# RWKV and gated delta cores: the inverse of the triangular blocks mirrored, with Y and X^T products on all four quarters of the array

## What is computed

```python
def step(state, inp):
    r_t, w_t, k_t, v_t, kk_t, b_t = inp
    sk = jnp.einsum('bhvk,bhk->bhv', state, kk_t)
    state = (state * w_t[:, :, None, :] - sk[..., None] * b_t[:, :, None, :]
             + v_t[..., None] * k_t[:, :, None, :])
    return state, jnp.einsum('bhvk,bhk->bhv', state, r_t)
```

```python
lower = jnp.where(strict, jnp.einsum('bhnid,bhnjd->bhnij', kb, k) * decay, 0.0)
tinv = lax.linalg.triangular_solve(eye + lower, eye, left_side=True, lower=True, unit_diagonal=True)
u = tinv @ (v * beta[..., None])
w = tinv @ (kb * jnp.exp(gcum)[..., None])
def step(S, inp):
    qd, kd, ui, wi, ai, gl = inp
    v_new = ui - wi @ S
    o = qd @ S + ai @ v_new
    S = S * gl[..., None, None] + jnp.einsum('bhcd,bhce->bhde', kd, v_new)
    return S, o
```

## Time and profile before

| | |
|---|---|
| median of 3 runs | 3152.23 us (3150.76 to 3156.98) |
| span of the profiled execution | 3153.8 us |
| PE busy / PEld busy | 2975.0 us (94%) / 2086.0 us (66%) |
| DVE / ACT / POOL busy | 1542.3 / 588.5 / 865.3 us |
| RWKV core | about 1036 to 1310 us of the span |
| gated delta core | about 2308 to 2515 us of the span |
| L2154, inverse products of RWKV | 3072 records, 115.4 us busy, 227 ns each |
| L3243, those of gated delta | 2688 records, 92.7 us busy, 222 ns each |

### The profile page before, as it was taken

How to read it: one execution, slowest core, us unless ns; L and a number is a source line. 1 busy time by engine, 2 the same in 40 slices (tenths; PEclk the granted TensorE clock), 3 DMA queues, 4 the chain that set the end, 5 groups by cost and what they waited for, 6 DMA issues and landing times. The chain is left out here.

```text
span 3153.8 us, 52317 instructions
## 1 busy us (share of the span) xinstructions
PE 2975.0 (94%) x22150; PEld 2086.0 (66%) x22150; DVE 1542.3 (49%) x2520; ACT 588.5 (19%) x1102; POOL 865.3 (27%) x591
## 2 busy tenths in 40 slices
PE   9999999999999899999999998999879998999998
PEld 6845857986887688658566685677768844443433
DVE  5764756336555467534777664764644332111112
ACT  2142040012001333210100002221443211110101
POOL 1111222111121545211899790011245310000000
PEclk9999999999999899999999999999999998999999
DMA  4342223220321000042334452132200017999996
GB/s 165 94 165 77 80 82 113 81 80 28 127 87 47 3 3 4 36 135 74 126 127 148 155 164 80 56 102 68 74 9 3 22 60 271 381 409 409 409 409 272
DMA packets 122230, 412.64 MB, mean 131 GB/s; under 512 B 13568, under 2 KB 21376, under 8 KB 121744
## 3 DMA queue, kind: packets, MB, share of 16 engines
q1 hardware_dynamic: 112784, 373.64, 33.3%
q0 software_dynamic: 9216, 35.66, 3.4%
HBM read 404.97 MB, written 4.28 MB: 130 GB/s over the span
## 5 line engine op out<-in xcount | busy, mean ns | idle before, releaser
L947 PE MATMUL ps<-arena 128*128 128x256 f32 x4760 | 1044.3, 381 | 18.0 <-PEq L905 6.8
L947 PEld LDWEIGHTS ps<-arena 128*128 128x128 f32 x4760 | 898.8, 191 | 173.9 <-issue 43.9
L1003 PE MATMUL ps<-arena 128*128 128x512 f32 (+1 forms) x752 | 291.5, 546 | 10.4 <-DVE arena L1342 7.3
L885 POOL TENSOR_TENSOR arena<-arena 128x512 f32<-128x512 f32 x68 | 94.1, 1384 | 555.9 <-DVE arena L903 190.5
L1003 PEld LDWEIGHTS ps<-arena 128*128 128x128 f32 x752 | 144.3, 193 | 149.6 <-issue 138.7
L3895 PE MATMUL ps<-arena 128*64 128x512 f32 x1024 | 224.8, 594 | 9.7 <-DMA arena<-in_w_up 7.2
L891 POOL TENSOR_TENSOR arena<-arena 128x512 f32<-128x512 f32 x68 | 86.5, 1271 | 484.7 <-PE ps L947 484.7
L1247 DVE TENSOR_TENSOR arena<-ps,arena 128x256 f32<-128x256 f32 x85 | 36.1, 425 | 331.1 <-PE ps L947 330.1
L1178 DVE SCALAR_TENSOR_TENSOR arena<-ps,params,arena 128x511 f32<-128x511 f32 (+4 forms) x266 | 190.7, 717 | 13.5 <-ACT arena L1079 4.4
L4039 POOL TENSOR_SCALAR arena<-arena,small 128x1024 f32<-128x1024 f32 x64 | 191.5, 2992 | 10.1 <-DMA arena<-in_w_mod 6.4
L3895 PEld LDWEIGHTS ps<-arena 128*64 128x64 f32 x1024 | 83.7, 137 | 149.2 <-issue 148.8
(11 more groups left out here) (453 smaller groups left out, 4047.6 us busy)
## 6 DMA issues: line engine op xcount, KB each, us to landing
arena<-in_w_in SPq DMA_DIRECT2D x166, 512.0 KB, 3.7
arena<-in_w_gate SPq DMA_DIRECT2D x128, 512.0 KB, 15.5
arena<-in_w_up SPq DMA_DIRECT2D x128, 512.0 KB, 15.3
arena<-in_w_down SPq DMA_DIRECT2D x128, 512.0 KB, 15.4
arena<-in_w_mod POOLq DMA_DIRECT2D x48, 512.0 KB, 4.2
arena<-in_ffn_up SPq DMA_DIRECT2D x44, 512.0 KB, 4.0
arena<-in_w_branch SPq DMA_DIRECT2D x32, 512.0 KB, 3.6
arena<-spill POOLq DMA_DIRECT2D x16, 640.0 KB, 5.3
```

The lines of the kernel that those rows point to most:

```text
L885: vec.tensor_tensor(plane(u, n), part(u, 1, 0), part(u, 1, 1), ALU.add).then_inc(sem, 1)
L947: last = nc.tensor.matmul(k.bank(b)[:, 0:HT], lhs[:, q * P:(q + 1) * P], rhs[:, q, :], start=(first and q == 0), stop=(q == 3), skip_group ...
L1003: last = nc.tensor.matmul(out[0:j["m"], 0:j["n"]], w[:, q * m:(q + 1) * m], j["rhs"](q), start=(n == 0), stop=(n == kn - 1))
```

## The change

In both cores the product is mirrored: a level now makes Y from XT, not from X, and XT from X and Y; X from Y and X. The order in a level is Y, XT, X. Y and XT (with X0, Y5 and XT5) are written so that the eight cells of one half of the partitions go to both halves and to two banks (`to_heads`, `to_chunks`; `to_tiles` in the gated delta core), round all four quarters. X (`in_heads`, `in_tiles`) stays on two, and takes a bank of its own: bank 6 in RWKV, which the norms, the turn of O and the bonus product use, with new waits between them and X; bank 7 in gated delta, where `chunk_u` moves too, with waits for X before each `chunk_u` and for its reader before X. The other steps there have banks 2, 3 and 4, and Y5, XT5 and X0 take two of them. RWKV's LT product is made twice, once each way round (banks 2 and 3, columns 0 to 255 and 256 to 511), since both orientations are wanted; in gated delta the LT step goes and an XT0 step comes. Readers of two banks read them in one instruction (`pair`, `both`). RWKV's turn of O moves from beat 10 to 9, the weighing from 12 to 10, the bonus from 14 to 13, its reader from 15 to 14; Y5 comes ahead of trv, which moves to beat 1, trkap from 2 to 4, trkt from 4 to 5.

The diff, cut to its core:

```diff
--- before.py
+++ after.py
@@ rwkv_core_phase
-    A = ["X0"] + [f"{s}{n}" for n in (1, 2, 3, 4) for s in ("Y", "X", "XT")]
-    B = ["trv", "Y5", "trkap", "XT5", "Lk", "trkt", "LkV", "trbt", "NU0", "WT", "Ak", "Ab"]
-    B_BEAT = [0, 0, 2, 2, 3, 4, 5, 6, 6, 7, 9, 11]
-    B_BANKS = [(3,), (2,), (3,), (2,), (2, 3), (3,), (2,), (3,), (2,), (2, 3), (2, 3), (2, 3)]
+    A = ["X0"] + [f"{s}{n}" for n in (1, 2, 3, 4) for s in ("Y", "XT", "X")]
+    B = ["Y5", "trv", "XT5", "Lk", "trkap", "trkt", "LkV", "trbt", "NU0", "WT", "Ak", "Ab"]
+    B_BEAT = [0, 1, 2, 3, 4, 5, 5, 6, 6, 7, 9, 11]
+    B_BANKS = [(2, 3), (2,), (2, 3), (2, 3), (2,), (3,), (2,), (3,), (2,), (2, 3), (2, 3), (2, 3)]
+    X_BANK = 6
     LT_BEAT = 13
+    TURN_BEAT, WEIGHED_BEAT, BONUS_BEAT, ADDED_BEAT = (9, 7), (10, 12), (13, 11), (14, 15)
@@
-            def blocks64(l, r, b):
-                for h in range(2):
+            def to_heads(l, r, b):
+                for i in range(TT):
+                    for q, h in ((0, 0), (1, 1), (0, 1), (1, 0)):
+                        other = k.const("ident")[half(q), half(q)] if r is None else r[half(q), cell(h, i)]
+                        ins = nc.tensor.matmul(k.bank(b + q)[half(h), 64 * i:64 * i + 64], l[half(q), cell(h, i)], other, start=True, stop=True)
+                return ins
+
+            def to_chunks(l, r, b):
+                for i in range(TT):
+                    for h, q in ((0, 0), (1, 1), (0, 1), (1, 0)):
+                        t = turned_cell(q, i)
+                        ins = nc.tensor.matmul(k.bank(b + h)[half(q), 64 * i:64 * i + 64], l[half(h), t], r[half(h), t], start=True, stop=True)
+                return ins
+
+            def in_heads(l, r, b):
+                for q in range(2):
                     for i in range(TT):
-                        for q in range(2):
-                            other = k.const("ident")[half(q), half(q)] if r is None else r[half(q), cell(h, i)]
-                            ins = nc.tensor.matmul(k.bank(b)[half(q), cell(h, i)], l[half(q), cell(h, i)], other, start=True, stop=True)
+                        for h in range(2):
+                            t = turned_cell(q, i)
+                            ins = nc.tensor.matmul(k.bank(b)[half(h), t], l[half(h), t], r[half(h), t], start=True, stop=True)
                 return ins
@@ step_a
-                    pe.wait_ge(*a_out(p, f"X{n - 1}"))
-                    ins = blocks64(LM(p), X(p), b)
+                    pe.wait_ge(*a_out(p, f"XT{n - 1}" if n > 1 else "X0"))
+                    ins = to_heads(LM(p), XT(p), 0)
...
-                    ins = blocks64(Y(p), XT(p), b)
+                    ins = to_chunks(X(p), Y(p), 0)
...
-                    ins = blocks64(XT(p), Y(p), b)
+                    if n == 1:
+                        pe.wait_ge(kap_ok, min(p + 2, PAIRS))
+                        if p >= 1:
+                            pe.wait_ge(*a_out(p - 1, "X4"))
+                    else:
+                        pe.wait_ge(*a_out(p, f"X{n - 1}"))
+                    if p >= 3 and n == 3:
+                        pe.wait_ge(weighed, p - 2)
+                    if p >= 3 and n == 4:
+                        pe.wait_ge(bonus_ok, p - 2)
+                    ins = in_heads(Y(p), X(p), X_BANK)
@@ step_lt
-                products(pl(a + p), pl(sg + p), 2).then_inc(lt_made, 1)
+                products(pl(a + p), pl(sg + p), 2)
+                products(pl(sg + p), pl(a + p), 2, 256).then_inc(lt_made, 1)
@@ the loop of PE
-                    if b >= 4 and beat == (10 if b < BLOCKS - 1 else 7):
+                    if b >= 4 and beat == TURN_BEAT[b == BLOCKS - 1]:
                         pe.wait_ge(norm_ok, b - 3)
                         pe.wait_ge(kap_ok, min(b + 1, PAIRS))
+                        pe.wait_ge(*a_out(min(b - 1, PAIRS - 1), "X2" if b < PAIRS + 1 else "X4"))
...
                         turn(O(b - 4), 6, k.const("swap")).then_inc(turned, 1)
-                    if b >= 4 and beat == (14 if b < BLOCKS - 1 else 11):
+                    if b >= 4 and beat == BONUS_BEAT[b == BLOCKS - 1]:
                         pe.wait_ge(weighed, b - 3)
                         pe.wait_ge(rk_ok, 2 * (b - 3))
+                        if b < PAIRS + 1:
+                            pe.wait_ge(*a_out(b - 1, "X3"))
                         nc.tensor.matmul(k.bank(6), HS, SQ(b - 4), start=True, stop=True).then_inc(bonus_in, 1)
@@ DVE, step_a and step_lt
+                if s[1] == "T":
+                    nc.vector.tensor_tensor(pair(x), pair(x), both(0), ALU.subtract).then_inc(a_dve, 1)
+                else:
+                    nc.vector.tensor_tensor(x, x, k.bank(X_BANK), ALU.subtract).then_inc(a_dve, 1)
...
-                nc.vector.tensor_tensor(quad(LT(p)), two_banks(2), mask(strict), ALU.mult).then_inc(lt_read, 1)
+                nc.vector.tensor_tensor(quad(XT(p)), two_banks(2), mask(first_level), ALU.mult)
+                nc.vector.tensor_tensor(quad(LS(p)), two_banks(2, 256), mask(after), ALU.mult).then_inc(lt_read, 1)
                 dve.wait_ge(lt_read, p + 1)
-                link(nc.vector.scalar_tensor_tensor(out=eight(XT(p)), in0=eight(LT(p)), scalar=-1.0, in1=mask8(level(0)), op0=ALU.mult, op1=ALU.mult))
-                nc.vector.tensor_tensor(eight(XT(p)), eight(XT(p)), mask8(ident), ALU.add).then_inc(lt_out, 1)
+                nc.vector.tensor_tensor(eight(XT(p)), mask8(ident), eight(XT(p)), ALU.subtract).then_inc(lt_out, 1)
@@ gdn_phase
+    X_BANK = 7
-    A = [f"{s}{n}" for n in (1, 2, 3, 4) for s in ("Y", "X", "XT")]
+    A = [f"{s}{n}" for n in (1, 2, 3, 4) for s in ("Y", "XT", "X")]
-    PREPARE = {0: ["R"], 4: ["KK"], 7: ["LT"], 9: ["QK"], 12: ["X0"]}
+    PREPARE = {0: ["R"], 4: ["KK"], 9: ["QK"], 10: ["XT0"], 12: ["X0"]}
+    TWO_BANKS = ("W", "Y5", "XT5", "X0")
-    BANKS = (2, 3, 7)
+    BANKS = (2, 3, 4)
-        n = 2 if step[0] == "W" else 1
-        banks_of[step] = [BANKS[(turn + i) % 3] for i in range(n)]
+        choices = ((2, 3), (3, 4)) if step[0] in TWO_BANKS else ((2,), (3,), (4,))
+        idle_since = lambda banks: max(ORDER.index(last_user[b]) if b in last_user else -1 for b in banks)
+        banks_of[step] = min(choices, key=idle_since)
@@ SP
+            sp.wait_ge(m_made, made_at("XT5", 4))
@@ step_a, X
+                    if n > 1:
+                        pe.wait_ge(*a_out(f"X{n - 1}", g))
+                    elif g >= 1:
+                        pe.wait_ge(*a_out("X4", g - 1))
+                    if g >= 3 and g % 2 == 1:
+                        pe.wait_ge(vn_ok, 4 * ((g - 3) // 2) + n)
+                    ins = in_tiles(X_BANK, Y(g), X(g))
@@ chunk_u
+                g = 2 * u + 3
+                if g < GROUPS:
+                    pe.wait_ge(*(a_out(f"X{n}", g) if n else a_out("X4", g - 1)))
+                elif n == 0:
+                    pe.wait_ge(*a_out("X4", GROUPS - 1))
-                        ins = nc.tensor.matmul(k.bank(4)[rows(z), wide(h)], ...
+                        ins = nc.tensor.matmul(k.bank(X_BANK)[rows(z), wide(h)], ...
```

More of the change, by code:

```diff
@@ L2027, in rwkv_core_phase @@
     own = lambda n: pl(at_plane[n])
-    LT, LM, X, XT, Y = (lambda p, n=n: own(5 * (p % 2) + n) for n in range(5))
+    LS, LM, X, XT, Y = (lambda p, n=n: own(5 * (p % 2) + n) for n in range(5))
     KT_, BT_, VT, NU, AK, AB = (lambda p, n=n: own(10 + 6 * (p % 2) + n) for n in range(6))
@@ L2138, in products @@
                         t = chunk(i, q)
-                        ins = nc.tensor.matmul(k.bank(b + h)[half(q), 64 * i:64 * i + 64], l[half(h), t], r[half(h), t], start=True, stop=True)
+                        ins = nc.tensor.matmul(k.bank(b + h)[half(q), at + 64 * i:at + 64 * i + 64], l[half(h), t], r[half(h), t], start=True, stop=True)
                 return ins
@@ L2386, in step_a @@
                 act.wait_ge(a_made, a_made_at(p, s))
-                nc.scalar.activation(Y(p) if s[0] == "Y" else X(p), k.bank(A.index(s) % 2), ACT.Copy).then_inc(a_act, 1)
+                nc.scalar.activation(pair(Y(p) if s[0] == "Y" else X(p)), both(0), ACT.Copy).then_inc(a_act, 1)
             def step_b(p, s):
@@ L3643, in _ @@
                         scaled(b - 2)
-                    if b < GROUPS and beat == 10:
+                    if b < GROUPS and beat == 8:
                         start(b)
```

163 lines of the change are left out of this document (96 added, 67 removed).

## The result

| | before | after |
|---|---|---|
| median, same chip and hour | 3156.61 us (3150.76 to 3161.19, 18 runs) | 3160.51 us (3153.80 to 3167.67, 18 runs) |
| ratio | | 1.0016, 95% interval 1.0008 to 1.0023 |
| span of the profiled execution | 3153.8 us | 3160.8 us |
| RWKV core, first scan to last gate product | 350.4 us | 366.3 us |
| gated delta core, first to last product that its function issues (its fills for the next phase among them) | 336.8 us | 322.9 us |

The change costs 5 us (2.5 to 7.3), which is inside the 0.2% that I had called "same", but on the other side of my forecast (2 us faster). Behind it stand two larger numbers of opposite sign. The windows of the profile after, answering, show them; columns as there. Blocks run from scan to scan of DVE in the RWKV core and from R product to R product in the other.

The account below looks back on a forecast made before the run. PE looked like the bound of both cores, though RWKV blocks change hands between ACT, DVE and PE. RWKV +8.1 and gated delta -11.0 gave -2.9, so 3152.2 became 3149.3; 0.7 for the clock made 3150 us, range 3133 to 3165.

Parts of the forecast that it names:

- same: Rival (a), whole kernel: the two cores' effects cancel, 3150 us, own range 3144 to 3157; chance 0.35.
- the last term of the sum: Whole kernel: more pauses of PE lower the clock, 0.7 us added to 3149.3.
- Rival (d): Full blocks and blocks 1 to 4: each loses one more half-clock stretch, 8 x 1.75 = 14 us, 3164; chance 0.19.
- six products x 0.38 less LT 0.62 and less a turn: RWKV block 2, behind the Lk mask: PE-bound saving of 1.1 us, the turn taken as 0.5.
- Beats 8 to 12: RWKV full block: turn of O, now in beat 9, waits for X2's subtraction, +1.15 us.
- Beat 12 to the results: RWKV full block: bonus product, now in beat 13, waits for X3's subtraction and delays LT, +2.3 us.
- The start of the block: RWKV blocks 5, 6, 7: later Y1 start (+0.4), product savings and a moved turn (+0.55) together give 0.0.
- rival (b): RWKV beats 8 to 15: earlier DVE subtraction hides the X2 and X3 waits, 14.5 us less, 3135; chance 0.32.
- my bounds of 1.8 to 3.3 for the second: Gated delta block 4: chunk_u's second wait for X's subtraction, behind DVE's XV and XK products, put at 2.5 us.
- (c): Rival, PE products: independent tiles bring a product to 0.50 us, another 8 us saved, 3142; chance 0.03.
- (e): Rival, gated delta: copies out of PSUM become the bound and its 11 us stay away, 3161; chance 0.06.
- (f): Rival, new products: they miss 0.63 us because operands lie differently; no saving, all waits stay, 3180; chance 0.05.

Follow-up runs that it names:

- gated delta alone: The kernel before with only the gated delta core of the changed kernel: 3147.42 us against 3154.95, ratio 0.9977.
- RWKV alone: The kernel before with only the RWKV core of the changed kernel: 3169.78 us, ratio 1.0047.
- output work moved only: The kernel before with only the turn of O, weighing, bonus product and its use moved to the changed kernel's beats, old products kept: 3165.61 us, ratio 1.0032.
- both back: The changed kernel with turn of O back in beat 10 (weighed in 11) and bonus product in 14 (used in 15): 3148.15 us, ratio 0.9973 to before.
- products in pairs: The changed kernel with matmuls of Y, XT and X0 going over two quarters at a time instead of four, both cores: 3185.21 us, ratio 1.0098 to before.
- second profile: The changed kernel run once more, unaltered, for its profile: 3151.38 us in this single run.
- the turn back: The changed kernel with only the turn of O back in beat 10 (weighed in 11), bonus product left in 13: 3155.75 us, ratio 1.0006 to before.

## Why the prediction was right or wrong

**The cause of the sign.** My sum was -2.9, +8.1 for RWKV and -11.0 for gated delta. In the profiles they are +15.9 and -13.9, in the timed runs of one core at a time +14.8 and -7.3. The mechanisms were those I named. What turned the sign is the clock, for which the sum had 0.7 us: the changed kernel stands at half clock for longer, and that costs 8 to 10 us.

**What half a clock costs.** Each execution on record has its mean clock beside its time, and within one kernel on one chip the two go together: over 153 executions of 12 such groups a mean clock 0.001 lower goes with 2.35 us more (0.12 standard error, correlation -0.85; one execution of before that took 6203.6 us is left out). 0.001 of 3155 us is 6.3 us at half clock, so each us at half clock goes with 0.37 us of time. No run set the clock, so this rests on executions that differ in it by themselves. Blocks that stand in two profiles, once with a stretch at half clock and once without, give the same: the old RWKV core at full clock has

```profile
1093.15:1125.39 32.24, 27.46 (x844) 24.57 (x840) 19.51 (x43) 9.39 (x17) 13.99 (x13) 1.00 0.02 4
1160.20:1193.86 33.66, 30.21 (x867) 26.55 (x868) 24.79 (x51) 12.75 (x21) 18.25 (x16) 1.00 0.01 4
```

for blocks 3 and 5 (profile of gated delta alone), where the kernel before had 34.76 at 0.90 and 35.05 at 0.95: 2.5 us for 6.8 at half clock, 1.4 us for 3.4. Block 4 of the gated delta core gives 1.4 for 3.4 and 2.7 for 6.8.

Now each kernel at the clock of before. This is an estimate: the measured difference less 2.35 us for each 0.001 of mean clock.

| kernel | mean clock, before's beside it | measured, us | at equal clock, us | forecast without the clock, us |
|---|---|---|---|---|
| gated delta alone | 0.9793, 0.9804 | -7.3 | -10 | -11.0 |
| RWKV alone | 0.9772, 0.9804 | +14.8 | +7 | +8.1 |
| whole change | 0.9764, see below | +5.0 | -3 to -5 | -2.9 |
| output work moved only | 0.9806, 0.9804 | +10.1 | +10.5 | |
| both back | 0.9764, 0.9804 | -8.5 | -18 | |

For the whole change the clock of before was not noted on its own chip; on three other chips it was 0.9804 to 0.9813, and its profiled execution had 0.980. The figures at equal clock are good to a us or two at best, on top of the intervals of the measured ones.

**The step that failed** is the last term of the sum, "with more pauses I add 0.7". Had that term been 8 to 10 us, the sum would have come out at +5 to +7, where the measured change is +5.0 (2.5 to 7.3). Rival (d) named this mechanism, one more stretch at half clock in a block, and I gave it 0.19. It asked for five blocks with one more; in the profiles the changed RWKV core has 17 us more at half clock, five stretches of 3.4, but in blocks 1, 6 and from 7 on, not in five blocks. It was too dear at 1.75 us for a stretch, where the rows above give 1.3 to 1.5, and it counted eight blocks where it named seven. Its sign, a clock below 0.93 in a full block, came in block 6 of both profiles (0.91), not in block 5 (0.95 and 0.94).

Why the clock falls is open. Moving the output work alone did not lower it (0.9806), though it adds waits. The mirrored kernel with its products in pairs has a low clock too (0.9768, before 0.9813), so the four-quarter order alone isn't it.

**A second step that failed, inside the RWKV sum.** By block (forecast, then measured from scan to scan):

| RWKV | forecast | measured | more us at half clock | |
|---|---|---|---|---|
| block 0 | +1.0 | +0.7 | 0.8 | |
| block 1 | -2.8 | -2.1 | 2.6 | |
| blocks 2 and 3 | -3.3 | +0.6 | 0.0 | PE's pauses |
| block 4 | +2.6 | +2.6 | 0.0 | |
| block 5 | +3.45 | +2.8 | 0.0 | |
| block 6 | +3.45 | +3.9 | 3.4 | |
| block 7 to the last gate product | +3.65 | +7.5 (+4.8 in the second profile) | 10.2 (3.4) | the clock |

It is "six products x 0.38 less LT 0.62 and less a turn" of blocks 2 and 3: I took it that PE, once it need not wait, runs as fast as its products. Both kernels have 6.8 us at half clock in these two blocks together, so the 3.9 us there are not the clock's. Two pauses of 1.18 and 1.51 us in block 2 and one of 0.29 in block 3 make 3.0 of them. I had even seen the products' 1.01 and 0.60 side by side, but never a stretch in which four or more fast ones follow each other, and the trace of before had none. Its nearest hint was there: packets of instructions 4 us apart in a trace whose PE needed 4 us for as many instructions. In the last row the two profiles of the changed kernel differ by 6.8 us at half clock and by 2.7 us of time; less 0.37 us for each us at half clock, the 7.5 become 3.7, which is the forecast. That the RWKV sum as a whole comes out so near at an equal clock is in part luck: blocks 1, 5 and 6 and block 0 were then 2.4 us cheaper than forecast, where blocks 2 and 3 were 3.9 dearer.

**The full blocks** were right in their size and nearly in their parts. Beats 8 to 12: +1.19 measured, +1.15 forecast. Beat 12 to the results: +1.88 against +2.3. The start of the block: from scan to beat 8 19.84 us against 20.65, -0.8 where I had 0.0. One part of that was the start of Y1, put at +0.4 by terms that add up to 5.3 and not to the 5.4 written; it came 4.97 us after the scan, before 4.93. The end, from the results to the next scan: +0.5 where I had nothing. The turn of v does wait for Y5's copy, 8 times, 4.9 us. Right in size but half wrong in reason: I put the beats' loss down to waits for X2 and X3. The moved places alone cost 2.2 a block with no wait for X at all; PE's two waits of 0.8 and 0.9 come on top, and the faster products about pay for those. So rival (b), waits hidden by a faster DVE, would not have brought 3135 even had it held.

**Gated delta** by block: 0 -1.1 (forecast -1.4), 1 -3.4 (-3.9), 2 -4.0 (-3.4), 3 -3.1 (-2.45), 4 +1.4 (+1.2), after that -3.7 (-1.1). PE waited for DVE's helper L3620, here X's subtraction, ahead of chunk_u eight times, 11.2 us in all with 3.3 the longest, at the upper of my bounds of 1.8 to 3.3 for the second. The moved chunk_u is right. What I had wrong is again the clock, in block 4 above all: the timed gain is 7.3 us, at an equal clock 10, forecast 11.

**Rivals (c), (e), (f).** (f) is out: 0.52 to 0.57 us a product. (e) is out: gated delta got faster. (c) was nearly right on a product alone, 0.52 us against its 0.50, but its gain of 8 us did not come. The rule of independent tiles (the Trainium skill, TensorEngine Tiling (Array Packing), Key Properties) is nearly met by such a product; in a row of eight, 0.77 us each, it is not.

## What to carry to other kernels

A piece of work that sits in a wait costs nothing; moved by one beat to make room for something else, it can cost its whole length. Price the place before the wait: here the places alone cost 10.1 us, on the old products and at the old clock, and putting two pieces back into their gaps (with the new buffers kept) turned +5 us into -8.5. Before a small difference is put down to the code, read the mean clock of every execution beside its time: here the clock was worth more than the whole forecast, and it hid half of the best kernel's gain. And when small matmuls are made faster, ask how many instructions a us the engine then eats; a pause inside a group that nothing releases, at the same place in every run, is the mark of it, and it can take back what was saved ahead of it.

## What the runs showed of the hardware

- **A ceiling for PE's instructions.** 512 instructions (eight products of 64x64 matmuls) took 6.1 us in four-quarter and 6.3 us in pair-wise order (means of six blocks, 5.5 to 7.3), with packets of 16 KB 3.4 to 4.7 us apart where I looked, and pauses that filled the difference. Shorter runs go at their own pace: 64 instructions in 0.52 to 0.57 us. All 77 unreleased pauses over 0.25 us in the RWKV cores stand at borders between pieces of 256 instructions.
- **The price of half clock.** 0.37 us of time for each us at half clock, over 153 executions; 0.37 to 0.43 from three blocks that stand in two profiles each.
- **The order of quarters and the number of banks.** The same 32 records take, from first to last matmul start, 0.93 us on the two diagonal quarters with one bank, 0.76 as two pairs with two banks, 0.48 round all four. In a row, pair-wise products take about 0.61 each (the row of 193 matmuls above, 3.88 us long), nearer to four quarters than to two. Order and banks changed together here, so their shares are not told apart. I had taken it that pairs are the old form; they are not.
- **Executions of one program differ by 14 us** here (3153.8 to 3167.7 for the changed kernel) and up to 21 in a variant (3146.8 to 3168.1 with the turn back), and the half-clock stretches, of 3.4 us or more, lie partly in other blocks each time. A block can be compared with a block only where both show the same clock.
